# Two modulation rows beside the mixer's projection, three between its attention products

## The reference

```python
def first_block(x, c, w_ada, b_ada, ...):
    cond = jax.nn.silu(c)
    for l in range(DEPTH):
        mod = cond @ w_ada[l] + b_ada[l]
        sh1, sc1, g1, sh2, sc2, g2, sh3, sc3, g3 = jnp.split(mod[:, None, :].astype(x.dtype), N_MOD, axis=-1)
        y = _swiglu(_modulate(x, sh1, sc1), ffn1_w_gate[l], ffn1_w_up[l], ffn1_w_down[l])
        x = _post_norm(x, y, g1, FFN_RES, ln_gain[l, 0], ln_bias[l, 0])
        y = _token_mixer(_modulate(x, sh2, sc2), w_in[l], w_out[l])
        x = _post_norm(x, y, g2, 1.0, ln_gain[l, 1], ln_bias[l, 1])
        y = _swiglu(_modulate(x, sh3, sc3), ffn2_w_gate[l], ffn2_w_up[l], ffn2_w_down[l])
        x = _post_norm(x, y, g3, FFN_RES, ln_gain[l, 2], ln_bias[l, 2])
    return x
```

## Time and profile before

| what | us |
|---|---|
| median of 3 runs (2630.8 to 2634.01) | 2632.61 |
| the profiled execution, its own time | 2631.91 |
| its span, first to last instruction | 2630.1 |
| mixer of layer 0, projection to the end of `values(5)` | 275.6 to 437.8 |
| mixer of layer 1, the same | 907.0 to 1065.4 |
| PE busy in the span | 2092.4 (80%) |

### The profile page before, as it was taken

The page is one execution under the profiler, slowest core; times in us unless marked ns, Lnnn a source line. Parts: engine busy times, 40 slices in busy tenths (PEclk is TensorE's granted clock), DMA queues, the critical chain, the costliest instruction groups (busy, mean ns, idle before and its releaser), DMA issues.

```text
span 2630.1 us, 34353 instructions
## 1 busy us (share of the span) xinstructions
PE 2092.4 (80%) x12924; PEld 1329.3 (51%) x12924; DVE 1023.6 (39%) x1644; ACT 526.2 (20%) x858; POOL 74.0 (3%) x108
## 2 busy tenths in 40 slices
PE   2999887899899898799979776666659867666665
PEld 1998345699799645499865421111117542111111
DVE  1787225688788613488733310000012230000002
ACT  1433122333333203233313200000001010000000
POOL 1000000000000000000100000000000000000000
PEclk6999897899899898899989788888889978888887
DMA  6896745688688584388760499999997369999996
GB/s 241 283 317 217 275 164 176 212 299 297 218 296 317 200 304 145 108 303 301 273 224 9 178 409 410 410 410 410 410 397 232 124 244 409 410 410 410 410 410 262
DMA packets 289438, 758.10 MB, mean 288 GB/s; under 512 B 17680, under 2 KB 125488, under 8 KB 289248
## 3 DMA queue, kind: packets, MB, share of 16 engines
q1 hardware_dynamic: 282368, 737.34, 74.7%
q0 software_dynamic: 6752, 19.79, 2.3%
q10 hardware_dynamic: 256, 0.13, 0.0%
HBM read 756.02 MB, written 1.18 MB: 288 GB/s over the span
## 4 chain that ended last, share of the span: by engine, by line
PE 57%; DMA 19%; SPq 13%; DVE 5%; issue 2%; ACT 2%; DVEq 1%; POOL 0%; ACTq 0%; POOLq 0%
PE psum L677 20%; DMA W<-in_w_exp_up 15%; SPq L471 11%; PE psum L689 9%; PE psum L740 6%; PE psum L717 4%; PE psum L1041 3%; PE psum L980 2%; PE psum L619 2%; DMA W_mod<-in_mod_w 1%; DMA W<-in_w_exp_down 1%; PE psum L882 1%; PE psum L650 1%; SPq L475 1%; ACT uT L1087 1%
## 5 line engine op out<-in xcount | busy, mean ns | idle before, releaser
L677 PE MATMUL psum<-parts 128*128 128x256 f32 x4224 | 528.8, 286 | 27.9 <-ACT parts L1077 20.6
L677 PEld LDWEIGHTS psum<-parts 128*128 128x128 f32 x4224 | 526.2, 195 | 35.5 <-issue 29.2
L980 PE MATMUL psum<-W,scr 128*32 128x512 f32 x2048 | 309.4, 705 | 189.5 <-DMA W<-in_w_exp_up 173.4
L980 PEld LDWEIGHTS psum<-W,scr 128*32 128x32 f32 x2048 | 50.7, 116 | 420.1 <-DMA W<-in_w_exp_up 341.2
L689 PE MATMUL psum<-parts 128*128 128x512 f32 x1056 | 257.8, 393 | 0.0
L1827 DVE TENSOR_TENSOR scr<-scr,psum 128x256 f32<-128x256 f32 x32 | 13.5, 421 | 583.0 <-ACT scr L1296 583.0
L1466 DVE TENSOR_TENSOR parts<-W,parts 128x1024 fp32r<-128x1024 f32 x176 | 207.5, 1222 | 67.3 <-ACT parts L1117 67.1
L1005 PE MATMUL psum<-W,scr 128*32 128x256 f32 x2048 | 168.0, 474 | 66.8 <-DMA W<-in_w_exp_down 49.9
L689 PEld LDWEIGHTS psum<-parts 128*128 128x128 f32 x1056 | 192.6, 188 | 45.3 <-DVE parts L1479 8.2
L1117 ACT ACTIVATE parts<-W 128x1024 fp32r<-128x1024 f32 x176 | 175.7, 1051 | 90.4 <-issue 46.9
L1346 DVE SCALAR_TENSOR_TENSOR mod_acc<-W_mod,cond,mod_acc 128x1024 f32<-128x1024 f32 x140 | 179.9, 1285 | 28.0 <-issue 27.7
(11 more groups left out here) (271 smaller groups left out, 1777.4 us busy)
## 6 DMA issues: line engine op xcount, KB each, us to landing
W_mod<-in_mod_w SPq DMA_DIRECT2D x128, 1024.0 KB, 6.1
W<-in_w_exp_down SPq DMA_DIRECT2D x128, 1024.0 KB
W<-in_w_exp_gate SPq DMA_DIRECT2D x256, 512.0 KB, 14.4
W<-in_w_exp_up SPq DMA_DIRECT2D x256, 512.0 KB, 15.7
W<-in_ffn_w_gate SPq DMA_DIRECT2D x44, 1024.0 KB, 9.3
W<-in_ffn_w_up SPq DMA_DIRECT2D x44, 1024.0 KB, 11.6
W<-in_ffn_w_down SPq DMA_DIRECT2D x44, 1024.0 KB, 9.1
W<-in_w_in SPq DMA_DIRECT2D x24, 1024.0 KB, 7.1
```

What stands on the lines that cost most here:

```text
L677: ins = pe.matmul(psum[:, 4 + t % 2, S * g:S * g + S], w[:, t % 2, g, kc, :], u[:, kc, :], start=(n == 0 and kc == 0), stop=(n == 2 and kc ...
L980: ins = pe.matmul(psum[32 * q:32 * q + 32, 4, :].rearrange("p (g n) -> p g n", g=2), xe_now[:, kc, :], w[:, :, q, :], start=(kc == 0), sto ...
```

## The change

In the mixer, r0 and r1 stay beside the projection (g = 1, 2). The row r2 leaves group g = 3, and r2, r3 and r4 share the attention steps b = 0 to 3, three quarters in each: r2 c0 to c2 in b = 0; r2 c3, r3 c0, r3 c1 in b = 1; r3 c2, r3 c3, r4 c0 in b = 2; r4 c1 to c3 in b = 3. SP's list, VectorE's `mixer_row` and ACT's `mod_row` follow.

```diff
@@ sync
+                def mix_chunk(n):
+                    mod_chunk(l * JOBS_LAYER + (FIRST_JOBS + PAIRS + n // 4), n % 4)
                 for u in range(MIX_USES):
                     s = MIX_S[u]
-                    if u >= 6:
-                        for c in (2 * (u % 2), 2 * (u % 2) + 1):
-                            mod_chunk(l * JOBS_LAYER + (FIRST_JOBS + PAIRS + (u - 6) // 2), c)
+                    if 6 <= u < 11:
+                        for c in (2 * (u - 6), 2 * (u - 6) + 1):
+                            mix_chunk(c)
...
+                for c in range(10, 4 * PAIRS):
+                    mix_chunk(c)
                 ffn_stream(l, 1)
@@ tensor, projection
-                            if kc == 3 and 1 <= g <= 3:
+                            if kc == 3 and 1 <= g <= 2:
...
-                        if 1 <= g <= 3:
+                        if 1 <= g <= 2:
@@ tensor, attention
                     if b < 4:
-                        for c in (2 * (b % 2), 2 * (b % 2) + 1):
-                            mod_quarter(l * JOBS_LAYER + (FIRST_JOBS + PAIRS + 3 + b // 2), l * PAIRS + (FIRST_JOBS + 3 + b // 2), c, bank=0)
+                        for c in range(3 * b, 3 * b + 3):
+                            mod_quarter(l * JOBS_LAYER + (FIRST_JOBS + PAIRS + 2 + c // 4), l * PAIRS + (FIRST_JOBS + 2 + c // 4), c % 4, bank=0)
                         second(b)
@@ scalar
-                    if n % 2 and 1 < n < 8:
+                    if n in (3, 5):
                         mod_row(l * JOBS_LAYER + (FIRST_JOBS + PAIRS + n // 2 - 1))
...
                 exps(2)
+                mod_row(l * JOBS_LAYER + (FIRST_JOBS + PAIRS + 2))
                 stick(1)
+                p_turned(2)
                 mod_row(l * JOBS_LAYER + (FIRST_JOBS + PAIRS + 3))
-                p_turned(2)
@@ vector
-                    for n in ((0, 1), (2,))[table]:
+                    for n in ((0, 1), ())[table]:
                         mixer_row(n)
...
                 dil_out(0)
+                mixer_row(2)
                 sticks(1)
-                mixer_row(3)
                 stick_mask(1)
                 weighted(2)
                 neg_abs(3)
                 stick_out(1)
+                mixer_row(3)
                 keeps(3)
```

## The result

| what | before | after |
|---|---|---|
| median (runs), same chip | 2631.98 | 2671.49 (2666.67 to 2678.83, 4 runs) |
| ratio to before, 95% interval | | 1.0152 (1.0123 to 1.018) |
| profiled execution, its own time | 2631.91 | 2678.83 |
| its span | 2630.1 | 2677.0 |

The change costs 39.5 us. A second set of four runs, which stands among the experiments, gave 1.0138 (1.0122 to 1.0155).

A forecast was written before the change was run, and what follows sets the result against it. PE was taken as the bound in the projection, and the time between `scores` and `values` as deciding attention. Projection -9.4, reload waits +34.3 and clock +4 gave +28.9 on 2631.91, so 2661 us, range 2648 to 2678.

The forecast's parts named there:

- the rival of the lower clock: Attention falls to the lower clock altogether, 24.9 us plus 20 for the upper bound, giving 2677 us; chance 0.12.
- The projection, -4.7 a mixer: Projection: PE is the bound, each quarter there costs 1.17 us, so moving r2's four gives back 4.7 us a mixer.
- the prediction's signs: Signs expected in the profile after; here, the last eight projection tiles without a quarter, 4.7 us shorter in each mixer.
- The reload: Attention b = 0 to 3: third chunk's load waits for the first quarter to free its buffer; +16.1 and +18.2 us.
- The estimate of 4.4 us: Skill's time for a 1 MB GpSimd transfer; with it eight waits were 0.6 us shorter each, sum about 24.
- the split wait: Attention b = 1: PE waits first for `mod_taken` of r2 (3.7 us), then r3 c1's landing; +5.2 and +4.9 us.
- the landing of 7.1 us: Attention b = 3: r4 c3's landing taken between 8.07 and 6.19 us; the step's term was +3.4 and +6.9 us.
- The clock, +2 a mixer: Attention: new waits of 4 to 5 us make more work after them slow; +2 us a mixer, +4 in all.
- the nearest row: Row behind the clock term: a quarter of 1.78 us and the slow `second` behind it, about 1.2 us at a step.
- The upper bound: Clock term's upper bound: all of attention at 1.2 GHz, some 10 us a mixer.
- `values(5)` would end 11 to 15 us later: Sign expected in the profile after, at the end of attention in each mixer, with nothing changed behind it.
- The rival of quarters in idle time: Four more quarters fill PE's idle times in attention, only the projection's 9.4 us gain remains, 2622.5 us; chance 0.04.

The follow-up runs named there:

- e1: The changed kernel with the third chunk of each step b = 0 to 3 loaded early into a free weight slot; 2635.36 us, ratio 1.0023 to before.
- e12: The changed kernel with third chunks early, next feed-forward weights held on SP, and POOL's column reads held until `values(3)`; 2625.4 us, ratio 0.9972 to before.
- half chunks: The changed kernel with the third chunk of b = 0, 1 and 2 loaded by half, 0.5 MB; 2646.98 us, ratio 1.006 to before.
- The filler: The changed kernel with products whose result nobody reads put into PE's wait ahead of each third quarter; 2651.86 us, ratio 1.0091 to before.
- e7: The changed kernel with third chunks early and the next feed-forward weights held on SP until r4 c2 is used; 2631.97 us, ratio 1.0001 to before.

## Why the prediction was right, and what it missed

It said 2661, range 2648 to 2678, and slower with 0.92; the median is 2671.5, in the range, with +39.5 us where the sum had +28.9. It is in the range only because that was widened for the rival of the lower clock: the forecast's own range ended at 2668, and both medians (2671.5, 2670.0) lie over it. Direction and place of the loss were forecast with reasons; a quarter of its size was not. Step by step:

**The projection, -4.7 a mixer: right.** From the first quarter to the last product it is 79.67 to 74.89 us in layer 0 and 79.92 to 74.89 in layer 1: -4.8 and -5.0. Each goes through the period of 4.63 against 3.46 us, which the rows of after repeat. The -5.4 and -3.2 of the table hold the pace of the first products (x40) and of the scores too, which the change didn't touch: x40 took 20.48 and 18.79 us in before, 19.85 and 19.59 in after. The tiles without quarters are the last six, not the last eight as the prediction's signs had it; the sum doesn't use that number.

**The reload: right in its place, and in its size partly by luck.** I had +16.1 and +18.2 for the steps without the clock; four quarters and the idle time give 4.0 + 12.1 = 16.1 and 4.0 + 13.4 = 17.4. But the working's own waits are larger. Ahead of the third quarters it has 4.1, 2.7 + 1.4, 4.1 and 6.8 us, with 0.99, 2.72 and 0.99 ahead of `values`: 23.8 us, or +13.8 and +15.2 over before, where +12.1 and +13.4 were measured. The 1.7 and 1.8 too much are the landing of b = 3. They don't show in the sum, because it sets every quarter and `second` at the full clock, also where before had slow ones (2.52 and 1.78 us in layer 0, 3.14 in layer 1); that took 1.7 and 1.0 us away unseen. Landings of b = 0 to 2 were taken as 5.0 and are 4.99 to 5.10. The estimate of 4.4 us that the Trainium skill allowed (DMA: Bandwidth & Descriptors, "Anatomy of one DMA — SWDGE (gpsimd) path") was too short for these transfers of SP's queue; here the measurement decides, and the row that the sum went by was the better guide. That three chunks in a row through two buffers are the cause, and not the number of the quarters, stands on the runs with the third chunks early and with quarters apart.

**b = 1: the split wait is as described.** `mod_taken` of r2 comes first: r3 c0 starts 3.62 us after r2 c3 (forecast 3.7), and the landing then takes 2.37 us more. "If c1 landed sooner, this would be the next wait" came true: 2.27 and 2.44 us with the third chunks early (e1, e12), 2.55 with half chunks.

**b = 3: the landing of 7.1 us was too long.** It is 5.39 and 5.21. I took the middle of 8.07 and 6.19 on the ground that the gate and up transfers still follow. What follows in the queue didn't lengthen it; in before c2 was in flight when c3 was issued, and in after it has landed. The term was 1.7 to 1.9 us too large a mixer, and in the total it is hidden by the full clock assumed elsewhere and by the clock term.

**The clock, +2 a mixer: the mis-sized term.** It is +11.5 a mixer in the first profile of the change and +6 in the second, and with the 1.7 and 1.0 us above the gap is larger still. The step that failed is the choice of "the nearest row": one slow quarter and its `second`, 1.2 us, once. What follows a wait isn't one quarter but `second`, `values` and `scores` too, and part of the quarters of the next step: in b = 2 and b = 3 two quarters take 3.04 and 3.06 us. The upper bound failed too: it was meant for all of attention at the lower level, and gave 10 us, since it added up four kinds of row instead of all of PE's work. The stage was never wholly at that level (PEclk 0.66), and 11.5 was reached. The whole stage could have been priced from the windows: 28.4 us busy at 0.82 are 23.3 us at full clock, with four quarters 27.3. Wholly at the lower level that is 54.6, 22 us over the 32.4 of before and four quarters, an upper bound that holds; at the 0.66 of the first profile, which nobody had ahead of the run, it is 41 us, against 43.9 measured. Because of this term the signs failed that `values(5)` would end 11 to 15 us later in each mixer: from the start of the projection it is 22 and 26 us.

**The rival of the lower clock** was given 0.12 and 2677 us. The first profile, 2678.83, is that case in size, and the median is nearer to it (5.5 us) than to the forecast (10.5); in kind it isn't, since PEclk in the stretch was 0.66 to 0.77 and not 0.50. The page named there (Trainium skill, TensorE: Matmul & The Clock Gate, "HAM oscillation — how this bites in real kernels") describes short groups of products that fall back at every landing wait. The rows of after agree in the main, with 1.93 instead of 1.07 us behind waits of 2.37, 4.20 and 4.93 us, but not at every wait: the quarter took 1.15 us behind 4.33 us, and in the second profile 1.07 us behind waits of 4.01 and 4.33 us. The filler shows the same by the opposite. It should have had more weight, or the forecast a larger clock term.

**The rival of quarters in idle time** (2622.5) fell for the reason given, a chunk can't be there in time. But its mechanism doesn't hold either: where the landing waits are nearly gone and PE's order is that of the change (e12), the four quarters still lengthen the stretch by 3.6 us in layer 0 at an idle time as before. That kernel is 7 us under before all the same, and where all of it lies is open: the turn behind `values(5)` (L672) starts 5.4 us earlier than in before in both layers (439.58 against 444.99, 1067.23 against 1072.62), and 1.5 of it stand ahead of the first mixer (274.07 against 275.59), so that layer 1 added nothing. No run holds the next weights in before, so their part isn't known.

**Range.** 2648 to 2678 holds both medians and seven of the eight runs of the change; 2678.83 is over it.

## What to carry to other kernels

Count the buffers against the uses that stand together in a queue: n uses in a row of n - 1 buffers cost one whole load at that place, whatever idle time there is elsewhere (5.0 to 5.4 us in each of four steps here, less what else PE had to do or wait for). Moving the uses apart took 46 to 47 us off, further buffers took 32 to 33, and 45 to 46 once the weights and POOL's reads no longer stood beside the loads, all by the differences to before: the two ways are worth about the same, and the first needs no memory. Where a change adds waits of some microseconds to a stage with short matmul groups, price the clock for all of PE's work of that stage, from its busy time and its PEclk, not for the one instruction behind the wait; in this case the clock was a third to a half of the damage (12 of 40 us in one profile, 23 of 47 in the other). If the wait can't be removed, the filler suggests that useful work put into it would be worth more than its own time; that wasn't measured.

## What the runs showed of the hardware

**Work that nobody needs can pay.** 14.5 us of filler in each mixer, put into waits, took 15 to 17 us from the execution, with PEclk in the stretch at 0.90 to 0.93 instead of 0.66 to 0.77.

**The same work at the same waits can take a different time.** Between the two profiles of the change the same 281 instructions differ by 6.2 and 4.7 us while the idle time agrees within 0.4. That the change varies more between executions than other kernels isn't shown: its eight runs spread over 13.4 us, and 29 runs of before over 13.0.

**Reads of single elements keep the DMA engines busy with few bytes.** POOL's four reads put two modulation rows and `ln_g`, `ln_b` into columns, 4 KB each, four bytes for each element. One takes 6.4 to 7.4 us to land. In before, layer 0, they are issued at 400.81 to 403.47. Two windows of before (columns as above):

```profile
406.00:408.00 2.00, 2.00 (x10) 1.91 (x10) 0.00 (x0) 0.00 (x0) 0.00 (x0) 0.50 1.02 201
408.00:410.00 2.00, 2.00 (x8) 1.73 (x6) 0.00 (x0) 0.00 (x0) 0.00 (x0) 0.50 0.99 226
```

With a chunk of r4, a `w_out` transfer and the reads in flight, the engines are full (DMA share 1.02 and 0.99) at 201 and 226 GB/s. With third chunks early and the weights held, and then with the reads held too, two windows ahead of the landing of r4 c2, one from each kernel (e7, then e12):

```profile
414.00:416.00 2.00, 0.98 (x16) 0.33 (x16) 1.91 (x2) 1.27 (x1) 0.00 (x0) 1.00 0.82 145
```

```profile
414.00:416.00 2.00, 2.00 (x17) 1.95 (x18) 0.00 (x0) 1.94 (x3) 0.00 (x0) 1.00 1.02 420
```

The chunk needs 9.98 us beside the reads and 7.27 without them, and PE's wait for it goes from 2.85 to 0.43 us (in layer 1 from 2.49 to none). It was worth 0.3% in this variant and nothing in the two others. Not every chunk suffers: in the change the reads are issued at 419.96, 1.7 us behind r4 c0, which still lands in 5.10 us.
